# Gated feed-forward rows: VectorE 32x32 block turns and sixteen SBUF-to-SBUF DMAs per block in place of eight TensorE transposes

## The chip, the cores and the metric

The kernel runs on one core of one Trainium2 chip. The metric is device time of one execution in microseconds (us). The core has TensorE (PE, matmuls), VectorE (DVE), ScalarE (ACT), GpSimd (POOL) and SyncE (SP, which here only issues DMAs); 16 DMA engines move data between HBM and the on-chip memory SBUF. PSUM is the memory that TensorE writes to.

## The reference

Two transformer-like blocks run one after another on 256 tokens of width 2048, all in fp32. The part that the change touches is the feed-forward (FFN) of the first block, which is called twice:

```
D_MODEL = 2048; SEQ = 256; D_FF = 5504
def rmsnorm(x, g):
    y = x32 * rsqrt(mean(x32 * x32, axis=-1) + EPS) * g
def swiglu(x, w_gate, w_up, w_down):
    return (silu(x @ w_gate) * (x @ w_up)) @ w_down
h = h + 0.5 * swiglu(rmsnorm(h, ffn1_norm), ffn1_w_gate, ffn1_w_up, ffn1_w_down)
...                       # an SSM mixer and a dilated attention, joined by w_out
h = h + 0.5 * swiglu(rmsnorm(h, ffn2_norm), ffn2_w_gate, ffn2_w_up, ffn2_w_down)
```

The second block (an mLSTM branch and an attention branch over 16 heads, with many projections) follows and is not touched. It takes a modulation vector silu(c) @ w_mod, which is computed on the side during the FFN stages of the first block.

## The kernel before

**Products.** Every fp32 product is made of three fp32r products: each operand is split into a rounded part (hi) and the rest (lo), and hi*hi, hi*lo and lo*hi are summed in PSUM. Weights stream through four slots. A chunk is 256 rows by 512 columns of a weight matrix (512 KB, seen as 128 partitions x 1024). For each chunk SP loads `w_raw` (line 221), ACT writes `w_hi` (line 239), DVE writes `w_lo` (line 246), and PE does 12 matmuls with it (lines 278 to 280: 2 k-tiles x 2 halves of the tokens x 3 products). There are 1060 chunks. SP may load chunk c when `w_lo` of chunk c-4 is done; ACT may write slot c when PE has used chunk c-4 (`w_used`). ACT and DVE stand LEAD = 4 chunks ahead of PE in the program, so when PE finishes chunk c-4, ACT rounds chunk c.

**One FFN.** The 5504 columns are cut into NB = 11 blocks of 512 (the last, block 10, has 384). For each block b PE does 8 gate chunks into `acc[:, 0]`, then 8 up chunks into `acc[:, 1]`. ACT writes `silu_gate` from the first, DVE multiplies both into `gated` (line 839; tokens on partitions, two halves h of 128 tokens). The down projection needs the gated rows with their columns on partitions (`g_hi`, `g_lo`), so they are turned: PE transposes the 8 (6 in block 10) 128x128 tiles of block b-1 into PSUM, `turned_tiles` (`turn_gated`, line 783), between chunks 7 and 8 of block b; ACT then writes `g_hi` (line 771) and DVE `g_lo` (line 775) from PSUM. Block 10 is turned in the down stage, ahead of its chunk TURN_AT = 4. The down stage has 4 x 22 chunks (lines 974 to 976), which reduce over all 43 column tiles.

**Order of each queue.** All engines run a fixed order. Blocks 0, 1, 9 and 10 are written out, blocks 2 to 8 are a loop (`Fori`). On DVE, chunk 3 of block b comes ahead of the two `gated` multiplications of block b-1, and chunk 4 after them. SP's queue holds the chunk loads only, in order. In most blocks of both FFNs POOL also loads eight 512 KB pieces of `w_mod` (line 698) into `mod_ring` and DVE adds them up (two operations of lines 711/714 after every second chunk, 16 in a block); PE sums them over partitions (line 723).

```
            def it(b, s, c, p, i, mod, last):      # ffn_sp: SP's queue in one block
                for m, w in enumerate((w_gate, w_up)):
                    for j in range(8):
                        load_chunk(sp, s + 8 * m + j, cols(w, 2 * j, b * BLK, width(b)), c + 8 * m + j)
```

Of the kernel before, what the change touches and what calls it, by code (L numbers as in the profile page):

```python
# [45 lines left out]
ACT = mybir.ActivationFunctionType  # L46
# [69 lines left out]
def build(nc, A, out):  # L116
    ctx = ExitStack()
    with ctx:
# [60 lines left out]
        gated = r("gated", [P, 2, BLK])  # L179
# [19 lines left out]
        g_turned, g_hi_done, g_lo_done = sem("g_turned"), sem("g_hi_done"), sem("g_lo_done")  # L199
# [548 lines left out]
        def ffn_sp(sp, name, w_gate, w_up, w_down, between=None):  # L748
            def it(b, s, c, p, i, mod, last):
                for m, w in enumerate((w_gate, w_up)):  # L750
                    for j in range(8):
                        if first(b) and m == 0 and between is not None:
                            between(sp, j)
                        load_chunk(sp, s + 8 * m + j, cols(w, 2 * j, b * BLK, width(b)), c + 8 * m + j)
            ffn_iterations(sp, name, it)
            s1 = AT[name][0] + 16 * NB
            wd = w_down.rearrange("(k p) n -> p k n", p=P)
            with sp.Fori(0, 2) as i:
                for j in range(2 * DOWN_CHUNKS):
# [7 lines left out]
        turned_tiles = pst[:, 0:2, :].rearrange("p a (b t) -> p (a b) t", b=2)  # L767

        def hi_tiles(act, n_use, b):
            act.wait_ge(g_turned, b + (NB * n_use + 1))  # L770
            act.activation(g_hi[:, tiles_of(b), :], turned_tiles[:, 0:width(b) // P, :], ACT.Copy).then_inc(g_hi_done, 1)

        def lo_tiles(dve, n_use, b):
            dve.wait_ge(g_hi_done, b + (NB * n_use + 1))
            dve.tensor_tensor(g_lo[:, tiles_of(b), :], turned_tiles[:, 0:width(b) // P, :],
                              g_hi[:, tiles_of(b), :].bitcast(F32), ALU.subtract).then_inc(g_lo_done, 1)

        def turn_gated(pe, n_use, b, p):
            pe.wait_ge(fetched[1], p + 2)
            pe.wait_ge(g_lo_done, b + (NB * n_use + 1))  # L780
            for t in range(width(b) // P):
                for h in range(2):
                    mm = pe.transpose(turned_tiles[:, t, h * P:(h + 1) * P],  # L783
                                      gated[:, h, t * P:(t + 1) * P], ident[:])
            mm.then_inc(g_turned, 1)
# [27 lines left out]
        def ffn_dve(dve, name, n_use, loaded=None):  # L813
            b0 = NB * n_use

            def it(b, s, c, p, i, mod, last):
# [21 lines left out]
                for h in range(2):  # L838
                    ins = dve.scalar_tensor_tensor(out=gated[:, h, 0:n], in0=acc[:, 1, h, 0:n], scalar=rstd[:, h:h + 1],
                                                   in1=silu_gate[:, h, 0:n], op0=ALU.mult, op1=ALU.mult)  # L840
                ins.then_inc(fetched[1], 1)
            ffn_iterations(dve, name, it)

        def ffn_pe(pe, name, n_use, turning):

            def it(b, s, c, p, i, mod, last):
# [8 lines left out]
                if not first(b):  # L855
                    turn_gated(pe, n_use, b - 1, p - 1)
# [4 lines left out]
        TURN_AT = 4  # L861
# [76 lines left out]
        def down_pe(pe, name, n_use, chained):  # L938
            s0, p0 = AT[name]
            s1 = s0 + 16 * NB  # L940
            pe.wait_ge(g_lo_done, NB * (n_use + 1))
            for q in range(4):
                if q % 2 == 0:
                    pe.wait_ge(fetched[q // 2], p0 + NB + 1)
                for j in range(DOWN_CHUNKS):
                    if q == 0 and j == TURN_AT:
                        turn_gated(pe, n_use, NB - 1, p0 + NB - 1)
                    if q == 0 and j == DOWN_CHUNKS - 2:
                        pe.wait_ge(g_lo_done, NB * (n_use + 1) + 1)
# [45 lines left out]
        def down_dve(dve, name, n_use, chained):  # L995
# [1965 lines left out]
        def _(dve):  # L2961
# [4 lines left out]
            dve.sem_inc(g_lo_done, 1)  # L2966
# [93 lines left out]
        def _(pool):  # L3060
# [132 lines left out]
```

## Time and profile before

| what | value |
|---|---|
| time, median of 3 runs | 3210.4 us (3208.71 to 3211.41) |
| the profiled execution's own time | 3210.79 us |
| its span in the profile | 3208.7 us |
| PE busy | 3178.2 us (99%) |
| DVE busy | 2062.4 us (64%) |
| ACT busy | 1475.7 us (46%) |
| POOL busy | 493.0 us (15%) |
| DMA | 655.37 MB, mean 204 GB/s |
| the `gated` transposes on PE (L783) | 172 matmuls |

The profile is of one execution. The span runs from its first to its last instruction; 2.1 us of the execution's own time lie around it. PE's queue is the bound where it is always busy; for the others the idle time and what ended it are read. Line numbers (L783) are those of the kernel before.

### The profile page before, as it was taken

To read this page: it belongs to the slowest core of one execution; us is meant where nothing else is said; L and a number is where in the kernel's file an instruction comes from. 1 tells how busy PE (TensorE), PEld (TensorE's weight loads), DVE (VectorE), ACT (ScalarE), POOL (GpSimd) and SP (SyncE) were. 2 spreads that over 40 slices of the span, in tenths; PEclk is the share of its full clock that TensorE was granted. 3 is DMA by queue.
4 is the path that set the end of the run, shared out by engine and by line. 5 is a ranking of instruction groups with operands and counts; after the bars stand their busy time and mean duration, and the time that the engine had idled before them with its cause. 6 is when DMAs were issued, how large, how long until landed. Compare 5 with 4: busy or idle time off the path is not lost.

```text
span 3208.7 us, 42304 instructions
## 1 busy us (share of the span) xinstructions
PE 3178.2 (99%) x15432; PEld 2626.3 (82%) x15432; DVE 2062.4 (64%) x2484; ACT 1475.7 (46%) x1834; POOL 493.0 (15%) x743
## 2 busy tenths in 40 slices
PE   8999999999999999999999999999999999999998
PEld 7888888888777888888988888888878877888886
DVE  6777775556886567777877564655665755445556
ACT  4444444445337444444445345545455554544443
POOL 1111116947660001111100000000000100000000
PEclk9999999999999999999999999999999999999999
DMA  7888886556443678888876555546866643665654
GB/s 244 279 275 276 280 260 198 199 189 199 146 147 100 210 226 277 281 276 280 274 257 220 190 188 179 177 140 178 162 151 186 189 133 103 177 198 181 211 185 151
DMA packets 317405, 655.37 MB, mean 204 GB/s; under 512 B 20872, under 2 KB 29328, under 8 KB 316608
## 3 DMA queue, kind: packets, MB, share of 16 engines
q1 hardware_dynamic: 290480, 555.91, 53.7%
q0 software_dynamic: 26768, 97.35, 12.5%
q8 instruction: 101, 1.65, 0.2%
q14 instruction: 56, 0.46, 0.0%
HBM read 647.93 MB, written 2.10 MB: 203 GB/s over the span
## 4 chain that ended last, share of the span: by engine, by line
PE 97%; DVE 1%; ACT 0%; issue 0%; POOL 0%; DMA 0%; SPq 0%; DVEq 0%; ACTq 0%; POOLq 0%
PE acc L278 24%; PE acc L280 24%; PE acc L279 24%; PE acc L974 2%; PE pst L974 2%; PE pst L976 2%; PE acc L976 2%; PE acc L975 2%; PE pst L975 2%; PE pst L2728 1%; PE pst L2710 1%; PE pst L2420 1%; PE pst L783 1%; PE pst L723 0%; PE pst L2422 0%; PE pst L1603 0%
## 5 line engine op out<-in xcount | busy, mean ns | idle before, releaser
L246 DVE TENSOR_TENSOR w_lo<-w_raw,w_hi 128x1024 fp32r<-128x1024 f32 x1060 | 1318.9, 1248 | 950.3 <-ACT w_hi L239 940.4
L239 ACT ACTIVATE w_hi<-w_raw 128x1024 fp32r<-128x1024 f32 x1060 | 1120.9, 1059 | 1444.9 <-PE acc L280 1148.5
L278 PE MATMUL acc<-w_hi,act_hi 128*128 128x512 f32 (+1 forms) x3360 | 1324.6, 394 | 4.1 <-DVE w_lo L246 4.0
L280 PE MATMUL acc<-w_hi,act_lo 128*128 128x512 f32 (+1 forms) x3360 | 1303.8, 388 | 0.0
L279 PE MATMUL acc<-w_lo,act_hi 128*128 128x512 f32 (+1 forms) x3360 | 1302.0, 387 | 0.0
L278 PEld LDWEIGHTS acc<-w_hi,act_hi 128*128 128x128 f32 x3360 | 631.5, 188 | 131.5 <-issue 9.0
L280 PEld LDWEIGHTS acc<-w_hi,act_lo 128*128 128x128 f32 x3360 | 631.2, 188 | 129.3
L279 PEld LDWEIGHTS acc<-w_lo,act_hi 128*128 128x128 f32 x3360 | 632.0, 188 | 122.4 <-issue 0.5
L698 POOL DMA_DIRECT2D mod_ring<-in_w_mod x160 | 115.9, 725 | 949.3 <-DVE pst L714 703.9
L714 DVE SCALAR_TENSOR_TENSOR pst<-mod_ring,c_act,pst 128x512 f32<-128x512 f32 x280 | 210.8, 753 | 5.5 <-DMA mod_ring<-in_w_mod 0.5
L974 PE MATMUL pst<-w_hi,g_hi 128*128 128x512 f32 x344 | 134.7, 392 | 0.0
L974 PE MATMUL acc<-w_hi,g_hi 128*128 128x512 f32 x344 | 134.7, 392 | 0.0
L976 PE MATMUL acc<-w_hi,g_lo 128*128 128x512 f32 x344 | 134.0, 390 | 0.0
L976 PE MATMUL pst<-w_hi,g_lo 128*128 128x512 f32 x344 | 134.0, 389 | 0.0
L975 PE MATMUL acc<-w_lo,g_hi 128*128 128x512 f32 x344 | 133.9, 389 | 0.0
L975 PE MATMUL pst<-w_lo,g_hi 128*128 128x512 f32 x344 | 133.8, 389 | 0.0
L2393 POOL DMA_DIRECT2D m_bc<-m_rows x16 | 8.6, 540 | 605.7 <-DVE g_col L2191 483.7
L976 PEld LDWEIGHTS acc<-w_hi,g_lo 128*128 128x128 f32 x344 | 64.6, 188 | 13.6
L976 PEld LDWEIGHTS pst<-w_hi,g_lo 128*128 128x128 f32 x344 | 64.6, 188 | 13.5
L975 PEld LDWEIGHTS pst<-w_lo,g_hi 128*128 128x128 f32 x344 | 64.6, 188 | 13.2
L975 PEld LDWEIGHTS acc<-w_lo,g_hi 128*128 128x128 f32 x344 | 64.6, 188 | 13.2
L974 PEld LDWEIGHTS pst<-w_hi,g_hi 128*128 128x128 f32 x344 | 64.6, 188 | 13.1
(463 smaller groups left out, 2431.9 us busy)
## 6 DMA issues: line engine op xcount, KB each, us to landing
w_raw<-in_w_in SPq DMA_DIRECT2D x400, 512.0 KB, 3.8
w_raw<-in_ffn_w_down SPq DMA_DIRECT2D x168, 512.0 KB, 3.9
w_raw<-in_ffn_w_gate SPq DMA_DIRECT2D x160, 512.0 KB, 4.9
w_raw<-in_ffn_w_up SPq DMA_DIRECT2D x160, 512.0 KB, 4.9
mod_ring<-in_w_mod POOLq DMA_DIRECT2D x160, 512.0 KB, 5.2
w_raw<-in_w_out SPq DMA_DIRECT2D x64, 512.0 KB, 4.2
w_raw<-in_w_branch_a SPq DMA_DIRECT2D x32, 512.0 KB, 3.9
w_raw<-in_w_branch_b SPq DMA_DIRECT2D x32, 512.0 KB, 4.6
```

The lines of the kernel that those rows point to most:

```text
L239: act.activation(weight_tiles(s)[0], w_raw[:, s % SLOTS, :], ACT.Copy).then_inc(w_hi_done, 1)
L246: dve.tensor_tensor(lo, w_raw[:, s % SLOTS, :], hi.bitcast(F32), ALU.subtract).then_inc(w_lo_done, 1)
L278: pe.matmul(o, xh, wh, start=k == 0, stop=False)
L279: pe.matmul(o, xh, wl, start=False, stop=False)
L280: mm = pe.matmul(o, xl, wh, start=False, stop=k == 2 * nch - 1)
L698: pool.dma_start(mod_ring[int(n >= 8 * MOD_PASSES["ffn2"])][n % 2][:].rearrange("p (k n) -> p k n", k=2), cols(A["w_mod_2"], 2 * (n % 8), ...
L714: ins = dve.scalar_tensor_tensor(out=mod_sum[:] if k == KT - 1 else part, in0=w, scalar=c, in1=part, op0=ALU.mult, op1=ALU.add)
L783: mm = pe.transpose(turned_tiles[:, t, h * P:(h + 1) * P], gated[:, h, t * P:(t + 1) * P], ident[:])
L974: pe.matmul(o, gh, wh, start=k == 0, stop=False)
L975: pe.matmul(o, gh, wl, start=False, stop=False)
L976: mm = pe.matmul(o, gl, wh, start=False, stop=k == FT - 1)
L2420: pe.matmul(o, decay[:, n % 2, st, th * P:(th + 1) * P], va[:, st, head, :], start=j == 0, stop=False)
```

## The change

The 172 PE transposes are gone. DVE's two multiplications write their product to PSUM (`pst[:, 0:2]`), and one DVE instruction (`turn_gated_dve`, a block transpose of 32x32 blocks) turns every 32x32 block within itself and writes `gated` in SBUF. The blocks are then on the wrong partitions: block (src, dst) of the 4 x 4 grid has to go from partition group src to group dst. Sixteen DMAs, issued by SP, do that (`move_gated_sp`), each from 32 partitions to 32 partitions, with 8 runs of 32 elements (128 bytes) on each partition (6 runs for block 10), 32 KB in all. They write `g_raw`, which lies on the same bytes as `g_lo`. ACT and DVE read `g_raw` in place of PSUM.

SP issues the sixteen moves of block b-1 between the loads of chunks 7 and 8 of block b, after a wait for DVE's turn; those of block 10 between the loads of chunks 7 and 8 of the down stage. DVE's turn waits for its own product and for the moves of the block before; ACT's `g_hi` waits for the moves. SP's loop over the down chunks is written out.

```diff
-        gated = r("gated", [P, 2, BLK])
+        gated = r("gated", [P, 4, 2, P])
+        g_raw = at("g_raw", [P, FT, SEQ], offset=stage0 + 4 * FT * SEQ)
...
                         load_chunk(sp, s + 8 * m + j, cols(w, 2 * j, b * BLK, width(b)), c + 8 * m + j)
+                    if m == 0 and not first(b):
+                        move_gated_sp(sp, n_use, b - 1)
...
-            with sp.Fori(0, 2) as i:
-                for j in range(2 * DOWN_CHUNKS):
-                    k, q = 2 * (j % DOWN_CHUNKS), j // DOWN_CHUNKS
-                    load_chunk(sp, s1 + j, wd[:, k:min(k + 2, FT), bass.ds(i * 1024 + q * BLK, BLK)],
-                               i * (2 * DOWN_CHUNKS) + s1 + j)
+            for q in range(4):
+                for j in range(DOWN_CHUNKS):
+                    load_chunk(sp, s1 + q * DOWN_CHUNKS + j, wd[:, 2 * j:min(2 * j + 2, FT), q * BLK:(q + 1) * BLK])
+                    if q == 0 and j == 7:
+                        move_gated_sp(sp, n_use, NB - 1)
...
+        GROUPS = P // 32
+        MOVED = 16 * GROUPS * GROUPS
+
+        def turn_gated_dve(dve, n_use, b, p):
+            done = b + NB * n_use
+            dve.wait_ge(fetched[1], p + 2)
+            if not (isinstance(done, int) and done == 0):
+                dve.wait_ge(g_moved, done * MOVED)
+            n = width(b)
+            dve.transpose(gated[:, 0:n // P, :, :].rearrange("p t h c -> p h t c"),
+                          pst[:, 0:2, 0:n].rearrange("p h (t c) -> p h t c", c=P)).then_inc(g_turned, 1)
+
+        def move_gated_sp(sp, n_use, b):
+            sp.wait_ge(g_turned, b + (NB * n_use + 1))
+            n = width(b) // P
+            for src in range(GROUPS):
+                for dst in range(GROUPS):
+                    o = g_raw[32 * dst:32 * dst + 32, tiles_of(b), :].rearrange("p t (h c) -> p (t h) c", h=2)
+                    i = gated[32 * src:32 * src + 32, 0:n, :, :].rearrange("p t h c -> p (t h) c")
+                    sp.dma_start(o[:, :, 32 * src:32 * src + 32], i[:, :, 32 * dst:32 * dst + 32]).then_inc(g_moved, 16)
...
         def hi_tiles(act, n_use, b):
-            act.wait_ge(g_turned, b + (NB * n_use + 1))
-            act.activation(g_hi[:, tiles_of(b), :], turned_tiles[:, 0:width(b) // P, :], ACT.Copy).then_inc(g_hi_done, 1)
+            act.wait_ge(g_moved, (b + (NB * n_use + 1)) * MOVED)
+            act.activation(g_hi[:, tiles_of(b), :], g_raw[:, tiles_of(b), :], ACT.Copy).then_inc(g_hi_done, 1)
...
-            dve.tensor_tensor(g_lo[:, tiles_of(b), :], turned_tiles[:, 0:width(b) // P, :],
+            dve.tensor_tensor(g_lo[:, tiles_of(b), :], g_raw[:, tiles_of(b), :],
                               g_hi[:, tiles_of(b), :].bitcast(F32), ALU.subtract).then_inc(g_lo_done, 1)
-
-        def turn_gated(pe, n_use, b, p):
-            pe.wait_ge(fetched[1], p + 2)
-            pe.wait_ge(g_lo_done, b + (NB * n_use + 1))
-            for t in range(width(b) // P):
-                for h in range(2):
-                    mm = pe.transpose(turned_tiles[:, t, h * P:(h + 1) * P],
-                                      gated[:, h, t * P:(t + 1) * P], ident[:])
-            mm.then_inc(g_turned, 1)
...
                 for h in range(2):
-                    ins = dve.scalar_tensor_tensor(out=gated[:, h, 0:n], in0=acc[:, 1, h, 0:n], scalar=rstd[:, h:h + 1],
+                    ins = dve.scalar_tensor_tensor(out=pst[:, h, 0:n], in0=acc[:, 1, h, 0:n], scalar=rstd[:, h:h + 1],
                                                    in1=silu_gate[:, h, 0:n], op0=ALU.mult, op1=ALU.mult)
                 ins.then_inc(fetched[1], 1)
+                turn_gated_dve(dve, n_use, b, p)
...
-                if not first(b):
-                    turn_gated(pe, n_use, b - 1, p - 1)
...
-        TURN_AT = 4
+        TURN_AT, MOVED_AT = 4, 7
...
-                    if q == 0 and j == TURN_AT:
-                        turn_gated(pe, n_use, NB - 1, p0 + NB - 1)
...
-                    if q == 0 and j == TURN_AT + LEAD:
+                    if q == 0 and j == MOVED_AT + LEAD:
                         hi_tiles(act, n_use, NB - 1)
```

The waits of `down_pe` on `g_lo_done` are one lower to match, and POOL's load of `ctx_nat`, which lies on `gated`'s bytes, waits for `g_moved` in place of `g_turned`.

SP's queue before, from block 9 on: gate loads and up loads of block 9, then of block 10 (384 columns), then the loop over the down chunks.

```order
L221 DMA w_raw<-in_ffn_w_gate 128x2x512 [waits w_lo_done] x8
L221 DMA w_raw<-in_ffn_w_up 128x2x512 [waits w_lo_done] x8
L221 DMA w_raw<-in_ffn_w_gate 128x2x384 [waits w_lo_done] x8
L221 DMA w_raw<-in_ffn_w_up 128x2x384 [waits w_lo_done] x8
L758 UNCONDITIONAL_BRANCH
L758 ISA
L221 ISA [waits w_lo_done]
L221 DMA w_raw<-in_ffn_w_down 128x2x512
L219 REGISTER_ALU
```

The same stretch now. Between the gate loads and the up loads of a block stand sixteen DMAs from `gated` to `g_raw`, the first of which waits for `g_turned`; in the down stage they stand behind eight loads.

```order
L222 DMA w_raw<-in_ffn_w_gate 128x2x512 [waits w_lo_done] x8
L793 DMA g_raw<-gated 32x8x32 [waits g_turned]
L793 DMA g_raw<-gated 32x8x32 x15
L222 DMA w_raw<-in_ffn_w_up 128x2x512 [waits w_lo_done] x8
L222 DMA w_raw<-in_ffn_w_gate 128x2x384 [waits w_lo_done] x8
L793 DMA g_raw<-gated 32x8x32 [waits g_turned]
L793 DMA g_raw<-gated 32x8x32 x15
L222 DMA w_raw<-in_ffn_w_up 128x2x384 [waits w_lo_done] x8
L222 DMA w_raw<-in_ffn_w_down 128x2x512 [waits w_lo_done] x8
```

Every up load of a block, and down chunk 8, has moved behind sixteen DMAs and behind a wait for DVE.

DVE's queue before at the end of block 1, the block ahead of the loop: chunk 3 of block 2 (`w_lo`), then the two multiplications that give `gated`, then the loop with chunk 4 of block 2.

```order
L714 SCALAR_TENSOR_TENSOR pst<-mod_ring_103,c_act,pst 128x512 [waits mod_used,mod_ready1]
L714 SCALAR_TENSOR_TENSOR mod_sum<-mod_ring_103,c_act,pst 128x512 [waits mod_used]
L246 TENSOR_TENSOR w_lo<-w_raw,w_hi 128x1024 [waits w_hi_done]
L839 SCALAR_TENSOR_TENSOR gated<-acc,token_norm,silu_gate 128x512 [waits g_turned,fetched_a,w_used]
L839 SCALAR_TENSOR_TENSOR gated<-acc,token_norm,silu_gate 128x512
L687 UNCONDITIONAL_BRANCH
L687 ISA
L246 TENSOR_TENSOR w_lo<-w_raw,w_hi 128x1024 [waits w_hi_done]
L704 ISA
L710 REGISTER_ALU [waits mod_ready0]
L711 TENSOR_SCALAR pst<-mod_ring_102,c_act 128x512 [waits mod_used]
```

The same place now: the product goes to `pst`, and a turn stands between it and the next `w_lo`.

```order
L715 SCALAR_TENSOR_TENSOR pst<-mod_ring_104,c_act,pst 128x512 [waits mod_used,mod_ready1]
L715 SCALAR_TENSOR_TENSOR mod_sum<-mod_ring_104,c_act,pst 128x512 [waits mod_used]
L247 TENSOR_TENSOR w_lo<-w_raw,w_hi 128x1024 [waits w_hi_done]
L856 SCALAR_TENSOR_TENSOR pst<-acc,token_norm,silu_gate 128x512 [waits g_turned,fetched_a,w_used]
L856 SCALAR_TENSOR_TENSOR pst<-acc,token_norm,silu_gate 128x512
L783 STREAM_TRANSPOSE gated<-pst 128x2x4x128 [waits g_moved,fetched_b]
L688 UNCONDITIONAL_BRANCH
L688 ISA
L247 TENSOR_TENSOR w_lo<-w_raw,w_hi 128x1024 [waits w_hi_done]
```

The `w_lo` of chunk 4 of the next block, on which SP's load of chunk 8 waits, now stands behind one more instruction.

## Rows read from the trace of the kernel before

**Rows 1.** The page: busy time of each engine; share of the chain.

```profile
PE 3178.2 (99%) x15432; PEld 2626.3 (82%) x15432; DVE 2062.4 (64%) x2484; ACT 1475.7 (46%) x1834; POOL 493.0 (15%) x743
...
PE 97%; DVE 1%; ACT 0%; issue 0%; POOL 0%; DMA 0%; SPq 0%; DVEq 0%; ACTq 0%; POOLq 0%
```

**Rows 2.** Waits of PE in total: engine, line, waited for, us, times, longest.

```profile
PE pst L518 <- DMA resid<-in_x: 6.0, 1, 6.0
PE acc L278 <- DVE w_lo L246: 4.0, 2, 3.7
```

**Rows 3.** Windows: us, busy time by engine, clock, DMA share, GB/s; FFN blocks.

```profile
131.00:174.50 43.50, 43.50 (x202) 36.21 (x201) 32.44 (x36) 17.18 (x18) 5.07 (x7) 1.00 0.88 276
```

**Rows 4.** The transposes of the gated rows by source line: ns min/median/max.

```profile
L783 PE MATMUL pst<-ident_sb,gated x172: 270/272/275, 82.4 to 1614.6; 128*128 128x128 f32 x172
```

**Rows 5.** ACT timeline in block 2 (start, us, operation, [idle before, releaser]).

```profile
127.98 1.06 ACT L239 ACTIVATE w_hi<-w_raw 128x1024 fp32r<-128x1024 f32 x1 [1.66 <-PE acc L280]
...
131.59 1.06 ACT L239 ACTIVATE w_hi<-w_raw 128x1024 fp32r<-128x1024 f32 x1 [0.48 <-PE acc L280]
134.31 1.06 ACT L239 ACTIVATE w_hi<-w_raw 128x1024 fp32r<-128x1024 f32 x1 [1.66 <-PE acc L280]
```

**Rows 6.** Timelines of DVE, SP and ACT: end of block 2, block 3 of ffn1.

```profile
152.86 1.40 DVE L839 SCALAR_TENSOR_TENSOR gated<-acc,token_norm,silu_gate 128x512 f32<-128x512 f32 x2
154.44 1.23 DVE L246 TENSOR_TENSOR w_lo<-w_raw,w_hi 128x1024 fp32r<-128x1024 f32 x1 [0.17 <-ACT w_hi L239]
...
155.69 20.38 SPq L221 DMA_DIRECT2D w_raw<-in_ffn_w_up  x8
...
173.35 1.06 ACT L239 ACTIVATE w_hi<-w_raw 128x1024 fp32r<-128x1024 f32 x1 [1.67 <-PE acc L280]
```

**Rows 7.** SP's chunk loads: issue time by source line, ns min/median/max.

```profile
L221 SPq FUSED_REGOPS  x688: 37/37/71, 89.6 to 3087.4; - x172
...
L221 SPq DMA_DIRECT2D w_raw<-in_ffn_w_up x176: 367/372/382, 23.9 to 1587.7; - x176
```

**Rows 8.** SP's first DMAs, issued with no wait between them.

```profile
0.74 0.39 SPq L2878 DMA_DIRECT2D ident_sb<-in_ident  x1
1.18 0.43 SPq L2879 DMA_DIRECT2D gains_sb<-in_gains  x1
1.66 0.43 SPq L745 DMA_DIRECT2D resid<-in_x  x1
...
5.90 0.49 SPq L745 DMA_DIRECT2D resid<-in_x  x1
```

**Rows 9.** DMA issues: KB each, median us from issue to landing.

```profile
w_raw<-in_ffn_w_up SPq DMA_DIRECT2D x160, 512.0 KB, 4.9
...
w_raw<-in_ffn_w_up SPq DMA_DIRECT2D x16, 384.0 KB, 3.9
...
ident_sb<-in_ident SPq DMA_DIRECT2D x1, 64.0 KB, 1.8
...
gains_sb<-in_gains SPq DMA_DIRECT2D x1, 32.0 KB, 1.8
```

**Rows 10.** DMA packets from 2.25 to 2.65 us, mostly the 256-byte rows of gains_sb.

```profile
DMA packets 142, 0.03 MB, mean 82 GB/s; under 512 B 142, under 2 KB 142, under 8 KB 142
...
q1 hardware_dynamic: 142, 0.03, 36.5%
```

**Rows 11.** DVE and ACT in block 10 of ffn1 (first two) and of ffn2.

```profile
470.62 1.40 DVE L839 SCALAR_TENSOR_TENSOR gated<-acc,token_norm,silu_gate 128x512 f32<-128x512 f32 x2
...
485.94 1.06 ACT L239 ACTIVATE w_hi<-w_raw 128x1024 fp32r<-128x1024 f32 x1 [1.02 <-PE acc L280]
...
1569.56 1.41 DVE L839 SCALAR_TENSOR_TENSOR gated<-acc,token_norm,silu_gate 128x512 f32<-128x512 f32 x2
...
1584.89 1.06 ACT L239 ACTIVATE w_hi<-w_raw 128x1024 fp32r<-128x1024 f32 x1 [1.02 <-PE acc L280]
```

**Rows 12.** DVE's subtraction from PSUM, by source line.

```profile
L775 DVE TENSOR_TENSOR g_lo<-pst,g_hi x22: 951/1224/1226, 87.2 to 1619.9; 128x1024 f32 x14, 128x1024 fp32r<-128x1024 f32 x6, 128x768 fp32r<-128x768 f32 x2
```

More of the change, by code:

```diff
@@ L198, in build @@
         nt_turned, nt_hi, nt_lo = sem("nt_turned"), sem("nt_hi"), sem("nt_lo")
-        g_turned, g_hi_done, g_lo_done = sem("g_turned"), sem("g_hi_done"), sem("g_lo_done")
+        g_turned, g_moved, g_hi_done, g_lo_done = (sem("g_" + n) for n in ("turned", "moved", "hi_done", "lo_done"))
         c_loaded, c_silu = sem("c_loaded"), sem("c_silu")
@@ L748, in ffn_sp @@
         def ffn_sp(sp, name, w_gate, w_up, w_down, between=None):
+            n_use = int(name == "ffn2")
             def it(b, s, c, p, i, mod, last):
@@ L764, in tiles_of @@
         def tiles_of(b):
             return slice(4 * b, min(4 * b + 4, FT)) if isinstance(b, int) else bass.ds(b * 4, 4)
-        turned_tiles = pst[:, 0:2, :].rearrange("p a (b t) -> p (a b) t", b=2)
+        GROUPS = P // 32
[8 more added lines that the diff above has]
+                          pst[:, 0:2, 0:n].rearrange("p h (t c) -> p h t c", c=P)).then_inc(g_turned, 1)
@@ L940, in down_pe @@
             s1 = s0 + 16 * NB
-            pe.wait_ge(g_lo_done, NB * (n_use + 1))
+            pe.wait_ge(g_lo_done, NB * (n_use + 1) - 1)
             for q in range(4):
@@ L945, in down_pe @@
                 for j in range(DOWN_CHUNKS):
-                    if q == 0 and j == TURN_AT:
-                        turn_gated(pe, n_use, NB - 1, p0 + NB - 1)
                     if q == 0 and j == DOWN_CHUNKS - 2:
-                        pe.wait_ge(g_lo_done, NB * (n_use + 1) + 1)
+                        pe.wait_ge(g_lo_done, NB * (n_use + 1))
                     if q and chained and j == TURN_AT:
@@ L1004, in down_dve @@
                     rest_chunk(dve, s1 + DOWN_CHUNKS * q + j)
-                    if q == 0 and j == TURN_AT + LEAD:
+                    if q == 0 and j == MOVED_AT + LEAD:
                         lo_tiles(dve, n_use, NB - 1)
@@ L2965, in _ @@
             dve.sem_inc(fetched[1], 1)
-            dve.sem_inc(g_lo_done, 1)
             dve.sem_inc(mod_added, 1)
@@ L3093, in _ @@
                 else:
-                    pool.wait_ge(g_turned, 2 * NB)
+                    pool.wait_ge(g_moved, 2 * NB * MOVED)
                 pool.dma_start(ctx_nat[:], A["ctx_2"].rearrange("(h p) d -> p h d", p=P)[:, h, :]).then_inc(cx_loaded, 16)
```

## The prediction

> **What bounds the kernel now.** I read the busy times and the chain first: PE is busy 99% of the span and holds 97% of the chain [rows 1]. Then PE's waits: of its two longest, one is for the first load of the input, and for `w_lo` it waited 4.0 us in all [rows 2]. So each microsecond of PE work taken away is a microsecond of time, as long as nothing else starts to hold PE. Then the window of one FFN block (43.5 us): PE fully busy, granted clock 1.00, DVE busy 32.4 us, ACT 17.2 us, the DMA engines 88% busy [rows 3]. DVE and ACT have room; DMA has little.
>
> **What goes.** There are 172 transposes [rows 4]: 20 groups of 8 and 2 of 6. Their duration of 272 ns overlaps, so the price is read from ACT, which rounds a chunk each time PE finishes one: 131.59 to 134.31 is an ordinary chunk, 2.72 us, and 127.98 to 131.59, with the transposes in it, is 3.61 us [rows 5]. A group of 8 costs 0.89 us, one transpose 0.111 us, all 172 of them 19.1 us. This is the whole possible gain. The rest of the change costs nothing on PE by itself; it can only take this back by making PE wait.
>
> **What is added, and what it can hold up.** The deadline is set by chunk 8 of each block, the first that SP loads behind the moves. In block 3 of ffn1 [rows 6]: DVE's product ends at 152.86 + 1.40 = 154.26. SP issued load 8 at 155.69. PE finished chunk 7 at 173.35 (ACT's rounding of chunk 11 was released by it), so `w_lo` of chunk 8 must be ready then. It now goes like this.
>
> - DVE's turn. No row shows one. The nearest is DVE's subtraction on the same 128x1024 elements from PSUM, 1.22 us [rows 12]; from below 0.95 us, its shortest form, from above two passes, 2.45 us. I take 1.22 us, one pass like the nearest row, and 0.1 us for the wait on its own product: it ends at 155.6. The product written to PSUM costs as before, and the `g_hi` and `g_lo` operations keep their sizes. The loss on DVE, 1.3 us in a block in which it is idle 11 us, is covered by that idle time: `w_lo` of chunk 4, at 154.44 before, slides to 155.6, and PE needs it eight us later.
> - SP waits for the turn (before, it went on at once with `w_lo`), then issues 16 moves at a pace m each. Queued behind are loads 8 to 15, and behind them ACT, DVE and PE.
> - Load 8 lands 4.9 us after its issue [rows 9], ACT takes 1.06, DVE 1.23 us, 0.1 us for hand-overs: 7.3 us.
>
> The room for the moves is 173.35 - 155.6 - 7.3 = 10.45 us: PE does not wait while m is below 0.65 us. In block 10 PE has only 3/4 of the work per chunk and the load is 384 KB, landing in 3.9 us [rows 9]. ffn1: product done 472.02, turn to 473.34, PE done with chunk 7 at 485.94 [rows 11]: room 485.94 - 473.34 - 6.3 = 6.3 us. ffn2: 1570.97, 1572.3, 1584.89 [rows 11]: the same 6.3 us. There m of 0.44 us is already too much. In the down stage PE's chunks are full ones again, while turn and moves are 3/4 as long, so the wait there comes last; I cost it at nothing: even at 0.77 us the moves, with three quarters of the packets, take 9.2 us, under the 10.45 of block 3, whose chunks are of the same length.
>
> **The pace m** decides. Bounds from rows: SP needs 0.37 us for one DMA and 0.04 for the register operation ahead of it [rows 7]; its first DMAs follow each other at 0.44 us [rows 8]. That is the lower end, 0.44. When full loads follow each other, seven intervals from 1.66 to 5.90 make 0.61 us each [rows 8]. Upper end: each move is 256 packets of 128 bytes and 16 semaphore writes. The only small packets of a weightless queue are the 256-byte rows of `gains_sb`: 142 packets in 0.40 us with the engines 36.5% busy [rows 10], so 272 would take 0.77 us if nothing overlaps. I take 0.61, since it is a row of whole DMAs in sequence on this queue with as many packets each, and lies between. With 0.61 the moves take 9.8 us.
>
> The sum is then: -19.1 (transposes) + 0 for the 18 ordinary blocks (9.8 against 10.45) + 2 x 3.5 for the blocks 10 (9.8 against 6.3) = -12.1 us. Against the profiled execution's own 3210.79 us (0.4 us above the median of the runs shown) that is 3198.7 us. With m = 0.44 it is -19.1 + 1.5 = 3193.2 us; with m = 0.77, each ordinary block waits 12.3 - 10.45 = 1.85 us and each block 10 6.0 us: -19.1 + 33.3 + 12.0 = +26.2, 3237.0 us. Above m = 0.65 time grows by 320 us for each us of m; gain and loss meet at m = 0.69.
>
> **Bytes.** One move's packets keep an engine busy for 16 x 16.4 ns (36.5% of 16 engines' 0.40 us over 142 packets [rows 10]) = 0.26 us at most if 128 bytes cost as much as 256, all sixteen 4.2 us a block, 10% of 43.5 us. With the 88% of [rows 3] that is 98%: just below full. I cost it at nothing, because part of the 88% is packets that wait for one another.
>
> **Rules of the Trainium skill.** What the rows show of the turn is only its neighbour of 1.22 us [rows 12]. The Trainium skill, "VectorE: DVE Perf Modes", The three transpose paths, gives 311 ns for a 128x128 bf16 turn on VectorE; as an estimate, eight of those are 2.5 us, which is near my upper end. By it each room shrinks by 1.2 us, ordinary blocks would wait 0.5 us and blocks 10 4.7 us, and the sum at m = 0.61 would be -19.1 + 9 + 9.4, or 3210 us. No row shows which is right.
>
> **The rivals.**
>
> 1. The moves are paced slower than the room (m of 0.7 or more), because the packets of one move do not overlap the next one's. PE then waits for `w_lo` of chunk 8 in every block: slower, 3237 us at m = 0.77, from m = 0.69 on. For it: [rows 10], engines 36.5% busy while small packets trickle. Against it: two small DMAs issued 0.44 us apart [rows 8] both landed in 1.8 us [rows 9], so they did not queue up.
> 2. The gain and the waits about cancel (m 0.67 to 0.71, or a two-pass turn): 3210 us.
> 3. The DMA engines become the bound in the FFN blocks: if a 128-byte packet on chip costs 1.6 times the 16.4 ns, the moves take 6.8 us, 16% of a block, and 88 + 16 = 104% makes each of 18 blocks 1.7 us longer: -19.1 + 31 = +12, 3223 us. It would show as PE waiting at several chunks of a block, not at chunk 8 alone. For it: 88% busy now. Against it: that share holds waiting.
> 4. The moves go one after another at their full landing time, 1.8 us for a small DMA [rows 9]: 28.8 us against a room of 10.45, 18 x 18.4 + 2 x 22.5 - 19.1 = +357, 3568 us. Against it stand the same two small DMAs that landed side by side. This is how the Trainium skill, "DMA: Bandwidth & Descriptors", Rules for kernel authors, would have one fear it: transfers under 64 KB pay mostly overhead. By that rule 32 KB moves are a poor trade; the trace agrees that a small DMA takes 1.8 us, but not that the next has to wait for it.
>
> **How the numbers follow.** Forecast (PE work gone, waits in blocks 10 only): 0.50, at 3199 us, own range 3192 to 3204. Rival 2: 0.12. Rival 1: 0.24. Rival 3: 0.09. Rival 4: 0.05. A measurement of this kernel can tell about 0.2% (6.4 us) from no change. Faster by more than that: 0.50; within: 0.14 (rival 2 and the near edge of 1 and 3); slower: 0.36. The range starts at the full gain, 3191.7, and must reach into the slower cases until a fifth is left out: over the 3237 of rival 1 and the 3223 of rival 3, to 3262 (m = 0.85); beyond are rival 4 and the far part of rival 1.
>
> **What would show it.** Right: no L783 matmul; PE's waits for `w_lo` with about 3 us in each block 10 and under 1 us in others; SP's sixteen issues filling about 10 us after the turn; DVE's turn at 1.2 us; load 8 issued about 10 us later than before, and ACT waiting for its landing, which is harmless up to PE's 173.35. Wrong: PE waiting for `w_lo` in each block (then m or the turn is mis-sized), or a turn over 2 us, or SP's issues slower than 0.65 us.

## The result and the profile after

The changed kernel is slower: 3238.2 us median (3236.0 to 3244.7, 4 runs) against 3209.6 us (3208.7 to 3211.4, 4 runs). The ratio is 1.0091, 95% interval 1.0079 to 1.0104. The forecast was 3199 us and faster; the time lies where rival 1 put it (3237 us). The span of the profiled execution went from 3208.7 to 3234.6 us, +25.9 us. Only fast executions are compared in this document; the one slow one, of e7, took 9977 us at a granted clock of 0.31 and is left out of e7's ratio.

The page of the changed kernel: busy times, and the chain of work that ended last.

```profile
PE 3170.8 (98%) x15260; PEld 2612.0 (81%) x15260; DVE 2071.5 (64%) x2506; ACT 1476.4 (46%) x1834; POOL 490.5 (15%) x743
...
PE 74%; SPq 7%; DMA 7%; DVE 6%; issue 3%; ACT 2%; POOL 0%; DVEq 0%; ACTq 0%; POOLq 0%
PE acc L279 18%; PE acc L281 17%; PE acc L280 17%; SPq L793 7%; DMA w_raw<-in_ffn_w_up 3%; PE pst L988 2%; PE pst L990 2%; PE pst L989 2%; DMA w_raw<-in_ffn_w_gate 2%; DVE w_lo L247 2%; PE acc L988 2%; PE acc L990 2%; PE acc L989 2%; ACT w_
```

PE still is busy 98% of the span, but it holds 74% of the chain, where it held 97% [rows 1]. SP's issues of the moves (L793) have 7% of it and the landing of DMAs another 7%. PE's waits, by line and releaser (us in total, times, longest):

```profile
PE acc L279 <- DVE w_lo L247: 32.8, 22, 5.1
...
PE acc L988 <- DVE w_lo L247: 4.2, 2, 2.8
```

They answer to [rows 2], where `w_lo` cost 4.0 us in two waits. The two waits of before are still there, so 33.0 us in 22 waits are new: 20 in the FFN blocks, one in each block from 1 to 10 of both FFNs, and 2 in the down stages. Why they are there is read in block 3 of ffn1: the timelines of DVE, SP, ACT and PE (start, duration, operation, [idle before, releaser]).

```profile
153.65 1.41 DVE L856 SCALAR_TENSOR_TENSOR pst<-acc,token_norm,silu_gate 128x512 f32<-128x512 f32 x2
155.19 1.25 DVE L783 STREAM_TRANSPOSE gated<-pst 128x1024 f32<-128x1024 f32 x1
156.36 1.18 DVE L247 TENSOR_TENSOR w_lo<-w_raw,w_hi 128x1024 fp32r<-128x1024 f32 x1
...
156.59 11.79 SPq L793 DMA_DIRECT2D g_raw<-gated  x16
168.57 13.17 SPq L222 DMA_DIRECT2D w_raw<-in_ffn_w_up  x8
...
172.72 1.06 ACT L240 ACTIVATE w_hi<-w_raw 128x1024 fp32r<-128x1024 f32 x1 [8.40 <-DMA w_raw<-in_ffn_w_up]
...
173.81 1.23 DVE L247 TENSOR_TENSOR w_lo<-w_raw,w_hi 128x1024 fp32r<-128x1024 f32 x1 [8.17 <-ACT w_hi L240]
...
175.09 0.50 PE L279 MATMUL acc<-w_hi,act_hi 128*128 128x512 f32 x1 [1.00 <-DVE w_lo L247]
```

The turn ends at 156.44. SP goes at once and is busy with the sixteen moves for 11.8 us; only then, at 168.57, is load 8 issued (155.69 in [rows 6]). ACT has been waiting 8.4 us when it lands, 4.1 us after its issue, DVE makes `w_lo` from 173.81 on, and PE waits 1.00 us. The move and the turn by source line (ns min/median/max):

```profile
L793 SPq DMA_DIRECT2D g_raw<-gated x352: 606/608/1486, 65.9 to 1644.2; - x176
L793 SPq FUSED_REGOPS  x224: 46/46/80, 110.4 to 1509.7; - x112
...
L783 DVE STREAM_TRANSPOSE gated<-pst x22: 983/1250/1253, 64.7 to 1633.4; 128x1024 f32<-128x1024 f32 x20, 128x768 f32<-128x768 f32 x2
```

SP needs 608 ns for the issue of a move, where a weight load takes 372 [rows 7]. In the loop, that is in seven blocks of each FFN, the moves follow each other at (11.79 - 0.61)/15, 0.745 us. The turn takes 1.25 us. The register operations (FUSED_REGOPS, 46 ns) stand in the loop only; in the parts that are written out SP is faster. Its bursts in block 10 and in the down stage of ffn1:

```profile
481.71 10.43 SPq L793 DMA_DIRECT2D g_raw<-gated  x16
...
521.36 11.19 SPq L793 DMA_DIRECT2D g_raw<-gated  x16
```

The first is a pace of (10.43 - 0.61)/15, 0.655 us.

One thing more is in the windows: four stretches of PE's lower level of clock (columns as in [rows 3]; the clock is 0.50 of full, so 1.2 GHz), which the kernel before does not have in these stages. The kernel before has one stretch of 3.4 us, in the second transformer-like block, which the changed kernel does not have.

```profile
362.20:365.40 3.20, 3.20 (x9) 2.47 (x8) 3.17 (x5) 2.97 (x5) 0.72 (x1) 0.50 0.84 209
495.30:501.90 6.60, 3.69 (x12) 3.72 (x13) 4.68 (x4) 5.87 (x7) 0.00 (x0) 0.50 0.84 271
1604.60:1611.20 6.60, 4.64 (x15) 4.67 (x16) 5.94 (x7) 5.75 (x8) 0.72 (x1) 0.50 0.71 225
1652.40:1655.60 3.20, 3.20 (x9) 2.53 (x8) 2.88 (x4) 1.06 (x1) 0.71 (x1) 0.50 1.00 398
```

### The profile page after: what moved, and what is told of

It is laid out like the page before. It is cut to its first block, busy times and chain, and to the rows that moved or that the text cites. A ratio compares the mean times of both kernels' runs of the same rounds, so it can differ in the third digit from the quotient of the medians.

```text
span 3234.6 us, 42032 instructions
## 1 busy us (share of the span) xinstructions
PE 3170.8 (98%) x15260; PEld 2612.0 (81%) x15260; DVE 2071.5 (64%) x2506; ACT 1476.4 (46%) x1834; POOL 490.5 (15%) x743
## 2 busy tenths in 40 slices
DMA packets 411101, 666.66 MB, mean 206 GB/s; under 512 B 114568, under 2 KB 123024, under 8 KB 410304
## 4 chain that ended last, share of the span: by engine, by line
PE 74%; SPq 7%; DMA 7%; DVE 6%; issue 3%; ACT 2%; POOL 0%; DVEq 0%; ACTq 0%; POOLq 0%
PE acc L279 18%; PE acc L281 17%; PE acc L280 17%; SPq L793 7%; DMA w_raw<-in_ffn_w_up 3%; PE pst L988 2%; PE pst L990 2%; PE pst L989 2%; DMA w_raw<-in_ffn_w_gate 2%; DVE w_lo L247 2%; PE acc L988 2%; PE acc L990 2%; PE acc L989 2%; ACT w_hi L240 2%; DVE pst L856 1%
## 5 line engine op out<-in xcount | busy, mean ns | idle before, releaser
L990 PE MATMUL acc<-w_hi,g_lo 128*128 128x512 f32 x344 | 134.5, 391 | 0.0
L990 PE MATMUL pst<-w_hi,g_lo 128*128 128x512 f32 x344 | 134.0, 389 | 0.0
L988 PEld LDWEIGHTS acc<-w_hi,g_hi 128*128 128x128 f32 x344 | 64.9, 189 | 18.2 <-DVE w_lo L247 5.1
L990 PEld LDWEIGHTS acc<-w_hi,g_lo 128*128 128x128 f32 x344 | 65.0, 189 | 13.8
L990 PEld LDWEIGHTS pst<-w_hi,g_lo 128*128 128x128 f32 x344 | 64.6, 188 | 13.5
```

The source lines that it names most:

```text
L988: pe.matmul(o, gh, wh, start=k == 0, stop=False)
L990: mm = pe.matmul(o, gl, wh, start=False, stop=k == FT - 1)
```

## The experiments

All times below are medians beside runs of the kernel before on the same chip (3210.8 to 3211.2 us). Two questions were put. What makes PE wait: SP's time for sixteen issues (theory A), or the 4096 small packets of a block on the DMA engines (theory B)? And what sets the issue time? e3, e4, e5 and e8 do not compute the whole result: in the first three the blocks are not carried across partitions, in e8 the gated rows are replaced by other data.

**e1: the moves spread.** Two moves behind each of the loads 8 to 15, in place of the burst; `g_hi` and `g_lo` are made some chunks later.

```diff
                         load_chunk(sp, s + 8 * m + j, ...)
-                    if m == 0 and not first(b):
-                        move_gated_sp(sp, n_use, b - 1)
+                        if m == 1 and not first(b):
+                            move_gated_sp(sp, n_use, b - 1, range(2 * j, 2 * j + 2))
...
-                    if q == 0 and j == 7:
-                        move_gated_sp(sp, n_use, NB - 1)
+                    if q == 0 and 8 <= j < 14:
+                        move_gated_sp(sp, n_use, NB - 1, range(3 * (j - 8), min(3 * (j - 8) + 3, 16)))
```

> The same moves and the same turn, but SP issues two moves after each of the loads 8 to 15 of a block (three after each of the down loads 8 to 13) in place of all sixteen behind load 7; g_hi and g_lo are made later in the block, when the moves are in. Theory A (SP's time: sixteen issues at 0.74 us in a row hold load 8 back by 11.9 us, and that alone makes PE wait): no load is held back by more than two issues, 1.5 us, which the room covers; PE's waits for w_lo fall from 38 us to about the 5 us of the kernel before, the whole 19.1 us of transposes is gained: 3209.6 - 19.1 = 3190 us, 3189 to 3195. Theory B (the 4096 small packets of a block load the DMA engines, which the weights need too): the packets are all there, PE goes on waiting, 3225 us or more. Theory C on the clock (TensorE falls to its lower level behind long waits only): no half-clock stretch in the FFN stages under A.

Measured: 3196.0 us (3194.0 to 3196.9, 5 runs), ratio 0.9955, interval 0.9941 to 0.9969. The packets on e1's page, the waits of PE, and SP's queue in one block:

```profile
DMA packets 411101, 666.66 MB, mean 209 GB/s; under 512 B 114568, under 2 KB 123024, under 8 KB 410304
...
PE acc L279 <- DVE w_lo L247: 4.0, 2, 3.7
...
PE acc L990 <- DVE g_lo L802: 2.1, 1, 2.1
...
154.44 0.37 SPq L222 DMA_DIRECT2D w_raw<-in_ffn_w_up  x1
154.99 1.41 SPq L794 DMA_DIRECT2D g_raw<-gated  x2
157.03 0.40 SPq L222 DMA_DIRECT2D w_raw<-in_ffn_w_up  x1
```

`w_lo` costs the 4.0 us of before and no more. Load 8 is out at 154.44, load 9 at 157.03. The changed kernel has the same 411101 packets on its page, so theory B falls, and SP's time is what made PE wait. The changed kernel's own burst says the same. This is its window from 156.60 to 168.40, columns as in [rows 3]:

```profile
156.60:168.40 11.80, 11.80 (x57) 9.87 (x57) 7.44 (x9) 3.19 (x3) 1.45 (x2) 1.00 0.68 177
```

While SP issues the sixteen moves the DMA engines are 68% busy and move 177 GB/s, against 88% and 276 GB/s over a block of before [rows 3]. e1 beats both kernels. Its one new wait (L990, 2.1 us, for `g_lo` at the start of the down stage of ffn2) comes from its own later `g_lo`, and a half-clock stretch of 3.4 us next to it costs some 1.7 us more; these are 3.8 of the 6 us by which it missed 3190, and the rest is not traced.

**e2: the burst behind load 9.** The sixteen moves stay together, two loads later.

```diff
-                    if m == 0 and not first(b):
+                        if m == 1 and j == 1 and not first(b):
...
-                    if q == 0 and j == 7:
+                    if q == 0 and j == 9:
```

> The burst of sixteen moves stays whole, but is issued behind load 9 instead of load 7 (behind down load 9 too). Theory A: the first load that is held back is then chunk 10, which PE needs two chunks (5.4 us) later, while the burst starts only some 2 us later than before, since SP is then let go by w_lo of chunk 5. In ordinary blocks load 10 is issued at about 170.5 on the clock of block 3, w_lo of chunk 10 is done at 178, and PE needs it at 178.8: no wait. In the blocks 10 (chunks of 2.08 us) it is still about 3 us late each. Sum -19.1 + 6 + at most 3 for the clock: 3197 to 3204 us. Theory B: place does not matter, within 5 us of 3238.

Measured: 3239.8 us (3237.1 to 3241.1, 4 runs), ratio 1.0093 (1.0078 to 1.0109). I was wrong, and with a number close to theory B's. Block 3 of ffn1 again, on SP, DVE, ACT and PE:

```profile
156.90 1.25 DVE L783 STREAM_TRANSPOSE gated<-pst 128x1024 f32<-128x1024 f32 x1
158.07 1.18 DVE L247 TENSOR_TENSOR w_lo<-w_raw,w_hi 128x1024 fp32r<-128x1024 f32 x1
160.62 2.47 DVE L247 TENSOR_TENSOR w_lo<-w_raw,w_hi 128x1024 fp32r<-128x1024 f32 x2
...
162.41 11.79 SPq L793 DMA_DIRECT2D g_raw<-gated  x16
174.38 9.43 SPq L222 DMA_DIRECT2D w_raw<-in_ffn_w_up  x6
...
149.09 1.06 ACT L240 ACTIVATE w_hi<-w_raw 128x1024 fp32r<-128x1024 f32 x1 [4.39 <-DMA w_raw<-in_ffn_w_gate]
178.51 1.06 ACT L240 ACTIVATE w_hi<-w_raw 128x1024 fp32r<-128x1024 f32 x1 [8.51 <-DMA w_raw<-in_ffn_w_up]
...
180.88 0.50 PE L279 MATMUL acc<-w_hi,act_hi 128*128 128x512 f32 x1 [1.10 <-DVE w_lo L247]
```

The burst began at 162.41, 4.3 us behind the end of the turn (158.15), where behind load 7 it began 0.15 us after it; I had expected it some 2 us later. Load 9 waits for `w_lo` of chunk 5, which stands on DVE behind the turn, `w_lo` of chunk 4 and two modulation operations, and ended at 161.8. The turn itself came 1.7 us later than in the changed kernel, since the backlog of the block before was still there: ACT waited 4.4 us for a gate load at 149.09. In all the burst began 5.8 us later, and the two chunks (5.4 us) that PE gave were used up. Moving the burst along the queue that it blocks gained nothing here; e1, with the same packets, shows that this is no verdict for the engines' load.

**e3 and e4: what the issue time hangs on, shape and packets.** In e3 each DMA has the same 256 packets of 128 bytes, but 128 partitions with two runs; in e4 each has 32 partitions with one run of 1 KB.

e3 (the moves of block 10 stay as they are):

```diff
+            if n == 4:
...
+                for u in range(4):
+                    for g in range(4):
+                        cs = slice(32 * g, 32 * g + 32)
+                        sp.dma_start(o[:, 2 * u:2 * u + 2, cs], i[:, 2 * u:2 * u + 2, cs]).then_inc(g_moved, 16)
+                return
```

e4:

```diff
-                    sp.dma_start(o[:, :, 32 * src:32 * src + 32], i[:, :, 32 * dst:32 * dst + 32]).then_inc(g_moved, 16)
...
+            w = 64 * n
+            for g in range(GROUPS):
+                for u in range(4):
+                    sp.dma_start(o[32 * g:32 * g + 32, w * u:w * u + w],
+                                 i[32 * g:32 * g + 32, w * u:w * u + w]).then_inc(g_moved, 16)
```

> Sixteen DMAs in the same place, each again 256 packets of 128 bytes, but from all 128 partitions to the same 128 partitions, two runs on each, where the kernel has 32 partitions with eight runs (in the 384-column blocks the moves stay as they are). The blocks are not carried across partitions, so this part of the computation is changed. Theory A1 (the issue time of 0.61 us, against 0.37 for a weight load with as many packets, comes from the form: 32 partitions, eight runs): SP's issue falls to about 0.37 to 0.44, the burst to 7 to 8 us, PE waits only in the blocks 10: about 3195 to 3200 us. A2 (it comes from on-chip source or small packets): issue stays 0.61, time stays near 3238. Theory B: 3238 whatever the issue.

Measured: 3239.7 us (3234.5 to 3245.2, 4 runs), ratio 1.0086 (1.0071 to 1.0102), as the changed kernel.

> Sixteen DMAs in the same place, each from 32 partitions to the same 32 partitions, with one run of 1 KB on each: 32 packets in place of 256, the same bytes (the blocks are not carried across partitions, so this part of the computation is changed). Theory A1 (form, that is runs per partition or number of packets): SP's issue falls to 0.44 or less, 3195 us. A2 (32 partitions as such, or the on-chip source): the issue stays at 0.61 and the time near 3238, though the packets are an eighth. Theory B (packets on the engines): time falls to 3195 though SP's issue stays at 0.61.

Measured: 3217.4 us (3210.8 to 3225.5, 10 runs), ratio 1.0023 (1.0014 to 1.0033). SP's issue in e3 by source line, then SP's issue of e4 and its burst in block 3:

```profile
L795 SPq DMA_DIRECT2D g_raw<-gated x320: 615/617/1417, 66.1 to 1607.8; - x160
...
L794 SPq DMA_DIRECT2D g_raw<-gated x352: 529/530/1782, 66.2 to 1625.5; - x176
...
158.46 10.51 SPq L794 DMA_DIRECT2D g_raw<-gated  x16
169.15 2.08 SPq L222 DMA_DIRECT2D w_raw<-in_ffn_w_up  x4
```

The issue stays at 617 ns with four times the partitions, so the shape is not the cause. With an eighth of the packets the issue takes 530 ns and the burst 10.5 us in place of 11.8, a pace of 0.665 us: the number of packets has a small part in the issue time. The time fell by 21 us for these 0.08 us, near the steepness that the prediction had (320 us for each us of pace would be 26).

**e8: the source in HBM.** Same destination, same shape, same packets, but read from the input x in HBM.

```diff
+                    i = A["x"].rearrange("r (a c) -> r a c", c=32)[32 * src:32 * src + 32, 8 * dst:8 * dst + 2 * n, :]
-                    sp.dma_start(o[:, :, 32 * src:32 * src + 32], i[:, :, 32 * dst:32 * dst + 32]).then_inc(g_moved, 16)
+                    sp.dma_start(o[:, :, 32 * src:32 * src + 32], i).then_inc(g_moved, 16)
```

> Sixteen DMAs in the same place with the same destination and the same 256 packets of 128 bytes, but the source is the input x in HBM in place of gated in SBUF (so the gated rows are replaced by other data). It tells what sets SP's issue time of 0.61 us. If the on-chip source: it falls to about 0.37 us, the pace to 0.45 us, and the time to about 3195 us. If the form or the small packets on the destination side: it stays 0.61 us, 3238 us.

Measured: 3201.2 us (3198.2 to 3203.0, 8 runs), ratio 0.997 (0.9959 to 0.9981). Issue time and PE's waits:

```profile
L794 SPq DMA_DIRECT2D g_raw<-in_x x352: 347/360/1468, 64.8 to 1606.8; - x176
...
PE acc L279 <- DVE w_lo L247: 9.3, 5, 3.7
```

360 ns, as a weight load, where the source in SBUF needs 608. The edit changes one thing more: the 1 KB that a move reads from a row of x lies in one piece, while in `gated` its eight runs lie apart. e4 helps here: its source is in SBUF and in one piece, with 32 packets in place of 256, and it still needs 530 ns. So at least the 170 ns between 360 and 530 go with the on-chip source; no run tells what the last 78 ns hang on beside the number of packets. SP's burst in block 3 is 7.92 us long, a pace of 0.504 us and not the 0.45 that I expected. The waits in the FFN blocks shrink to 5.3 us over those of before, 5.1 of it in the blocks 10; 1.7 us come in the down stage of ffn2. The kernel is faster than before. It is 6 us over what I expected, and two half-clock stretches of 3.4 us stand beside those waits.

**e5: four moves.** The same bytes in four DMAs of 128 partitions with a 1 KB run each.

```diff
-            for src in range(GROUPS):
-                for dst in range(GROUPS):
...
+            w = 64 * n
+            for u in range(4):
+                sp.dma_start(o[:, w * u:w * u + w], i[:, w * u:w * u + w]).then_inc(g_moved, 16)
```

> The same bytes per block in the same place, but in four DMAs of 128 partitions with one 1 KB run on each (four issues in place of sixteen; the blocks are not carried across partitions, so this part of the computation is changed). Theory A (the number of issues on SP): 4 x 0.55 to 0.66 us is 2.6 us at most, inside the room even of the blocks 10 (6.3 us); no wait is left, no half-clock stretch in the FFN stages: 3210.8 - 19.1 = 3192 us, 3190 to 3194. Theory D (the wait of SP for DVE's turn, or the turn itself, costs as well): something of 5 us or more stays, 3197 us or above.

Measured: 3192.8 us (3189.8 to 3193.6, 4 runs), ratio 0.9948 (0.9931 to 0.9964). PE's waits for `w_lo` are the 4.0 us of the kernel before:

```profile
PE acc L279 <- DVE w_lo L247: 4.0, 2, 3.7
...
154.47 2.46 SPq L793 DMA_DIRECT2D g_raw<-gated  x4
```

The burst is 2.5 us and holds nobody up. DVE's turn, SP's wait for it and the gated product written to PSUM are all in this kernel, and still the transposes are worth what the prediction gave them: 18.4 us by the medians, for 19.1. By the spans it is 20.8 us, of which 1.7 are the half-clock stretch of before, which e5 does not have. So the turn, the wait and the PSUM write cost next to nothing.

**e6: only the last moves spread.** Block 10 and the down stage as in e1, the other blocks as in the changed kernel.

```diff
-                    if m == 0 and not first(b):
+                        if m == 1 and not first(b) and isinstance(b, int) and b == NB - 1:
+                            move_gated_sp(sp, n_use, b - 1, range(2 * j, 2 * j + 2))
+                    if m == 0 and not first(b) and not (isinstance(b, int) and b == NB - 1):
                         move_gated_sp(sp, n_use, b - 1)
...
-                    if q == 0 and j == 7:
-                        move_gated_sp(sp, n_use, NB - 1)
+                    if q == 0 and 8 <= j < 14:
+                        move_gated_sp(sp, n_use, NB - 1, range(3 * (j - 8), min(3 * (j - 8) + 3, 16)))
```

> Moves issued in block 10 and in the down stage are spread as in e1; in the 18 ordinary blocks the burst stays behind load 7. In the changed kernel PE's five waits in the blocks 10 and the down stages are 13.5 us and three half-clock stretches of 17 us in all (8.5 us lost) stand with them. Theory C (the clock falls at the long waits only): both go, 3238.2 - 13.5 - 8.5 = 3216 us. If the clock falls at the short waits of ordinary blocks just as well, only 13.5 go: 3225 us.

Measured: 3229.4 us (3221.9 to 3234.1, 4 runs), ratio 1.0066 (1.0049 to 1.0083). The profiled execution has a span of 3220.0 us, 14.6 below the changed kernel's, and PE waits as follows:

```profile
PE acc L279 <- DVE w_lo L247: 22.1, 19, 3.7
...
PE acc L994 <- DVE g_lo L804: 2.0, 1, 2.0
PE acc L994 <- DVE w_lo L247: 1.8, 1, 1.8
```

22.1 us are the 4.0 of before and 18.1 us in the ordinary blocks, so the 9.2 us of the blocks 10 are gone. The down stages still have 3.8 us, both waits in ffn2, in place of 4.2. The median lies above both of my numbers and its four runs are 12 us apart, so this run doesn't settle what the clock adds.

**e7: the moves from POOL.** The same sixteen DMAs in one burst, out of POOL's queue; SP issues none.

```diff
+                if n % 8 == 2:
+                    p = n // 8
+                    move_gated_sp(pool, int(p > 8), p if p < 9 else p - 9)
                 if n >= 2:
                     pool.wait_ge(mod_used, 2 * n - 2)
...
-                    if m == 0 and not first(b):
-                        move_gated_sp(sp, n_use, b - 1)
...
-                    if q == 0 and j == 7:
-                        move_gated_sp(sp, n_use, NB - 1)
...
             mod_loads_pool(pool, 2, 8 * MOD_PASSES["ffn2"])
+            move_gated_sp(pool, 0, NB - 2)
+            move_gated_sp(pool, 0, NB - 1)
```

> The same sixteen moves per block, in one burst, but issued by POOL, ahead of the third w_mod load of a block, so that SP's chunk loads are not behind them. Theory A (SP's time): PE's waits for w_lo of chunk 8 go. POOL needs 0.72 us for a load, 11.6 us for the burst, by which the w_mod load behind it is late; DVE waits for that at its sixth chunk, but has 10 us until then: 3191 to 3200 us. Theory B (packets on the engines): waits stay, 3225 us or more.

Measured: 3208.2 us (3206.1 to 3210.8, 9 of 10 runs), ratio 0.9994 (0.9984 to 1.0004): no difference from the kernel before. PE's waits, and DVE at the start of the down stage of ffn1:

```profile
PE acc L279 <- DVE w_lo L247: 8.2, 5, 3.7
PE acc L987 <- DVE w_lo L247: 6.9, 1, 6.9
...
511.83 0.35 DVE L1014 RECIPROCAL ssm_par<-ssm_par 128x32 f32<-128x32 f32 x1 [11.83 <-POOL ssm_par L1406]
```

SP is free and the waits of ordinary blocks are gone but for 1.0 us, as theory A wants. But two waits are new. DVE's reciprocal in the down stage of ffn1 waits 11.8 us for a table that POOL makes behind the moves, four `w_lo` are behind it on DVE, PE waits 6.9 us, and from 508.9 to 518.9 the granted clock is 0.50. In block 10 of ffn2 PE waits 3.3 us: there DVE stood 6.4 us for a `w_mod` load that POOL issues behind the moves. A burst moved to another queue holds up what is behind it there. e7 says nothing on theory B, since the packets are not the same: its trace has none of 128 bytes, but sixteen of 2 KB for each move.

**e9: e1 with a later wait.** PE asks for block 9's `g_lo` ahead of down chunk 18, where it is first read.

```diff
-            pe.wait_ge(g_lo_done, NB * (n_use + 1) - 1)
+            pe.wait_ge(g_lo_done, NB * (n_use + 1) - 2)
...
+                    if q == 0 and j == DOWN_CHUNKS - 4:
+                        pe.wait_ge(g_lo_done, NB * (n_use + 1) - 1)
```

> As e1 (moves spread over the loads), and PE waits for block 9's g_lo ahead of down chunk 18, the first that reads it, and no longer ahead of down chunk 0. In e1 PE waited 2.1 us for that g_lo at the start of the down stage of ffn2, and a half-clock stretch of 3.4 us (1.7 us lost) stood with it. Both should go: 3196.0 - 2.1 - 1.7 = 3192 us, 3190 to 3195. If the wait only moves to another instruction of DVE (w_lo of the first down chunks, which stands in the same queue behind g_lo), the time stays at 3196 us.

Measured: 3194.6 us (3192.2 to 3196.5, 5 runs), ratio 0.9949 (0.9935 to 0.9963).

```profile
PE acc L279 <- DVE w_lo L247: 4.0, 2, 3.7
PE acc L992 <- DVE w_lo L247: 3.6, 1, 3.6
...
1620.30 1.55 DVE L715 SCALAR_TENSOR_TENSOR pst<-mod_ring,c_act,pst 128x512 f32<-128x512 f32 x2 [9.32 <-DMA mod_ring<-in_w_mod]
```

The wait for `g_lo` is gone and another has come a little later: DVE waits 9.3 us for a `w_mod` load, and PE 3.6 us behind it. The moves are behind this one too, by way of POOL, whose load of `ctx_nat` must wait until the last of them has landed (see The change), and whose next `w_mod` loads stand behind that:

```profile
1610.14 0.56 POOL L3112 DMA_DIRECT2D ctx_nat<-in_ctx  x1 [12.17 <-DMA g_raw<-gated]
```

In the changed kernel this wait of POOL is 5.2 us and in e5 there is none: spreading the moves also makes the last one late, and what waits for all of them pays. Against e1 the 1.4 us are within the spread of the runs. Of the versions that compute the whole result e1 and e9 are the fastest, some 15 us (0.5%) under the kernel before.

## Why the prediction was wrong

**What held.** PE was the bound and its transposes were worth 19.1 us: e5 has 18.4. The deadline was chunk 8, the first load behind the moves, and PE waits there. The turn takes one pass, 1.25 us for my 1.22. The estimate from the Trainium skill (VectorE: DVE Perf Modes, The three transpose paths), 2.5 us from its bf16 figure, is twice that, so the measurement decides. The load of the engines (rival 3) did not come: e1 has all the packets and no such wait. Nor did serial landing (rival 4): the moves landed in 2.5 us (median), while the next ones were being issued. One reading was loose and without effect: PE needed `w_lo` of chunk 4 of block 3 about 5.6 us after it was ready (173.35 less four chunks of 2.72 us is 162.5, against 156.8), not eight.

**The step that failed** is the term m, the pace of the moves, taken as 0.61 us for all of them. It measured 0.745 in the fourteen blocks of the loops and about 0.655 in the blocks 10. Two things are in the difference. The issue alone takes 608 ns, as much as I had given to issue and gap together. The value came from [rows 8], whole loads in sequence at the start, and the lower end from the issue time of loads out of HBM [rows 7]; none of those has its source in SBUF, and e8 shows what this left out, 360 ns against 608. And in the loop 0.137 us stand between two issues, where the lower end had 0.04 for a register operation; e8, whose issue is short, still has 0.504 us from one move to the next there. With the measured pace and my rooms, the fourteen blocks wait 1.47 us each, 20.6, and the blocks 10 wait 4.2 each, 8.4: -19.1 + 29.0 = +9.9 us, where I had -12.1. The waits measured in the FFN blocks are 28.8 us. That the total fits so well has luck in it. In block 3, load 8 is issued 12.1 us after the turn, but is there for ACT 4.15 us later and not 4.9, and PE waits 1.0 us and not 1.47; on the other side four written-out ordinary blocks wait 3.7 us together, where my rooms allow next to nothing, and two blocks of the first loop wait 2.2 and 2.7 us, which is not traced.

Rival 1 was right in its place: PE waits for `w_lo` of chunk 8 in every block. Its cause was wrong, since it is SP's own time and not packets that follow each other slowly, and its price of 3237 us was met by luck: its 0.77 us is above both measured paces, and terms that it did not have make up the rest. That the interval between the small packets of `gains_sb` [rows 10] gave 0.77, close to the pace in the loop, was not for the reason given either.

**Terms that were missing** make the other 16 us. The waits in the trace are 33.0 us: 19.6 in the 18 ordinary blocks, 9.2 in the blocks 10 and 4.2 in the down stages, which I had put at nothing. There I let the moves take 9.2 us at most, three quarters of 12.3, because they have three quarters of the packets. But SP's issue of a 24 KB move takes the same 606 ns, and the bursts took 11.2 us in ffn1 and 10.4 in ffn2. On top of that each wait costs the overlap of the matmuls. Rows of PE around one of them:

```profile
360.90 0.50 PE L279 MATMUL acc<-w_hi,act_hi 128*128 128x512 f32 x1 [2.66 <-DVE w_lo L247]
361.23 0.40 PE L280 MATMUL acc<-w_lo,act_hi 128*128 128x512 f32 x1
361.47 0.40 PE L281 MATMUL acc<-w_hi,act_lo 128*128 128x512 f32 x1
...
362.68 0.63 PE L279 MATMUL acc<-w_hi,act_hi 128*128 128x512 f32 x1
363.11 0.63 PE L280 MATMUL acc<-w_lo,act_hi 128*128 128x512 f32 x1
```

The next matmul starts 0.33 us after the first one behind the wait, where 0.23 is usual, and the last one ahead of a wait runs out its 0.39 us; together 0.26 us, in 22 waits an estimated 5.7 us. Then the half-clock stretches: a matmul starts each 0.43 us at 362.68, against 0.24 at 361.23. PE was busy for 14.7 us in the four windows shown, of which half, 7.4 us, is lost by estimate, less 1.7 us for the one stretch of before that is not in this kernel: 5.7 us net. The sum is -19.1 + 33.0 + 5.7 + 5.7 = 25.3 us of the 25.9. That the clock falls because PE stood still is argued from where the stretches are: two begin during waits of 5.1 and 4.1 us, two 0.9 and 1.3 us after the end of waits of 2.8 and 2.7 us. No run here changes the clock alone, and e1 has one stretch, from 2210.8, with no wait near it; sixteen transposes of 8x8 (1.95 us, from 2208.65) stand right ahead of it. So the low stretches are read from the trace, and their cause is not shown.

## What to carry to other kernels

A queue that feeds the bound has a deadline for its next load. Count what a new burst takes of the queue's own time (issues times the pace of this kind of DMA, source, destination and the loop around it included) and compare it with that deadline; bytes and packets can be harmless while issues are not. Here the moves, spread in twos and threes over gaps in which the queue would wait anyway, cost the loads nothing; the same issues in one piece did, at both places that were tried. Spreading has a price too: it makes the last move late, so look at what waits for all of them. If the pace of the new DMAs has no row, the forecast hangs on it, and a bound read from DMAs of another kind is no bound.

## What was unexpected

- A DMA from SBUF to SBUF takes SP 608 ns to issue, one with the same destination and the same packets from HBM 360 ns, and one from SBUF to SBUF with 32 packets in place of 256 530 ns. In the loop some 0.14 us come on top of each.
- POOL issues the sixteen moves in 9.0 us (0.57 us each) where SP needs 10.4 to 11.8, and in the trace each has sixteen packets of 2 KB in place of 256 of 128 bytes (in block 10, 1.5 KB).
- TensorE's lower level came in stretches of 3.4 and 6.8 us in the changed kernel, beside waits of 2.66 us and more, and not in e5, which has none of these waits. That is a pairing in these traces, not a rule that a run here tests; e1 has a stretch without such a wait.
